# Gated delta rule in a two-block fp32 model: three pairs' token transposes moved into the first substitution, key products into the gate chain, 64x64 turns, and the merge copies in another order

## The reference, cut to what matters

```python
decay = jnp.exp(jnp.where(incl, gcum[..., :, None] - gcum[..., None, :], -jnp.inf))
a_kk = jnp.where(strict, jnp.einsum("bhnid,bhnjd->bhnij", k_beta, k) * decay, 0.0)
t_inv = lax.linalg.triangular_solve(eye + a_kk, eye, left_side=True, lower=True, unit_diagonal=True)
u = jnp.einsum("bhnij,bhnjd->bhnid", t_inv, v * beta[..., None])
w = jnp.einsum("bhnij,bhnjd->bhnid", t_inv, k_beta * jnp.exp(gcum)[..., None])
qk = jnp.einsum("bhnid,bhnjd->bhnij", q, k) * decay
...
v_new = ui - jnp.einsum("bhcd,bhde->bhce", wi, state)
o = jnp.einsum("bhcd,bhde->bhce", qd, state) + jnp.einsum("bhcj,bhje->bhce", qki, v_new)
state = state * gt[..., None, None] + jnp.einsum("bhcd,bhce->bhde", kd, v_new)
```

## Time and profile before

| what | us |
|---|---|
| runs | median 3757.83 of three, lowest 3757.76 |
| profiled execution, its own time | 3760.46 |
| its span, first to last instruction | 3758.6 |
| granted clock of PE, mean over the span | 0.97 of full speed (2.4 GHz) |
| delta rule of layer 0, from the gates (331 us) to the recurrence's first product (457 us) | 126 |
| the same in layer 1 | 1300 to 1427 |

### The profile page before, as it was taken

The page is one execution under the profiler, slowest core; times in us unless marked ns, Lnnn a source line. Parts: engine busy times, 40 slices in busy tenths (PEclk is TensorE's granted clock), DMA queues, the critical chain, the costliest instruction groups (busy, mean ns, idle before and its releaser), DMA issues.

```text
span 3758.6 us, 49965 instructions
## 1 busy us (share of the span) xinstructions
PE 3586.9 (95%) x18796; PEld 2882.4 (77%) x18796; DVE 1716.3 (46%) x2670; ACT 978.1 (26%) x1732; POOL 1819.9 (48%) x1049
## 2 busy tenths in 40 slices
PE   7999799999999979999999999999999999999999
PEld 5776677878776757787887788888888789888887
DVE  5255645737434574564551164444434124344342
ACT  3235532201223464121121133232101124232110
POOL 5522235656553222566565534435656431535654
PEclk9999799999999969999999989999999999999999
DMA  3211012323231101222222311213223423212222
GB/s 118 87 48 32 24 57 84 100 85 99 86 95 51 51 1 46 90 90 95 89 95 90 110 36 57 73 52 98 101 84 96 112 87 94 79 56 89 101 89 90
DMA packets 80743, 292.88 MB, mean 78 GB/s; under 512 B 8520, under 2 KB 9672, under 8 KB 80456
## 3 DMA queue, kind: packets, MB, share of 16 engines
q1 hardware_dynamic: 78496, 283.82, 23.7%
q10 hardware_dynamic: 1032, 2.62, 0.6%
q0 software_dynamic: 1056, 4.19, 0.3%
HBM read 281.69 MB, written 8.91 MB: 77 GB/s over the span
## 4 chain that ended last, share of the span: by engine, by line
PE 80%; DVE 9%; ACT 4%; issue 4%; DMA 1%; POOL 1%; DVEq 0%; ACTq 0%; SPq 0%; POOLq 0%
PE PSUM L337 19%; PE PSUM L336 19%; PE PSUM L335 19%; PE PSUM L896 2%; PE PSUM L1881 1%; PE PSUM L898 1%; PE PSUM L897 1%; DVE PSUM L494 1%; PE PSUM L1885 1%; DMA SLABS<-w_k 1%; PE PSUM L951 1%; DVE ACT_HI L1772 1%; PE PSUM L1459 1%; PE PSUM L908 1%; PE PSUM L1418 1%
## 5 line engine op out<-in xcount | busy, mean ns | idle before, releaser
L288 POOL TENSOR_TENSOR W_LOS<-SLABS,W_HI 128x1024 fp32r<-128x1024 f32 (+2 forms) x454 | 1157.7, 2550 | 37.9
L286 POOL TENSOR_SCALAR W_HI<-SLABS 128x1024 fp32r<-128x1024 f32 (+2 forms) x454 | 511.7, 1127 | 1316.6 <-DMA SLABS<-w_k 1316.6
L336 PE MATMUL PSUM<-H_LO,W_HI 128*128 128x512 f32 x2480 | 982.5, 396 | 0.0
L335 PE MATMUL PSUM<-H_HI,W_HI 128*128 128x512 f32 x2224 | 883.4, 397 | 26.1 <-DVE H_LO L479 20.9
L337 PE MATMUL PSUM<-H_HI,W_LOS 128*128 128x512 f32 x2224 | 884.7, 398 | 0.0
L336 PEld LDWEIGHTS PSUM<-H_LO,W_HI 128*128 128x128 f32 x2480 | 467.7, 189 | 118.2 <-issue 2.4
L335 PEld LDWEIGHTS PSUM<-H_HI,W_HI 128*128 128x128 f32 x2224 | 419.0, 188 | 131.8 <-issue 21.9
L337 PEld LDWEIGHTS PSUM<-H_HI,W_LOS 128*128 128x128 f32 x2224 | 418.5, 188 | 98.1
L494 DVE TENSOR_TENSOR PSUM<-PSUM,FACTORS 128x512 f32<-128x512 f32 x282 | 195.2, 695 | 554.0 <-PE PSUM L337 491.4
L335 PE MATMUL PSUM<-ACT_HI,W_HI 128*128 128x512 f32 x928 | 370.5, 399 | 13.0 <-DVE H_LO L455 6.4
L337 PE MATMUL PSUM<-ACT_HI,W_LOS 128*128 128x512 f32 x928 | 372.0, 401 | 0.0
(11 more groups left out here) (499 smaller groups left out, 5048.5 us busy)
## 6 DMA issues: line engine op xcount, KB each, us to landing
SLABS<-w_k SPq DMA_DIRECT2D x422, 512.0 KB, 3.5
SLABS<-w_k SPq DMA_DIRECT2D x32, 768.0 KB, 4.3
SLABS<-w_k SPq DMA_DIRECT2D x32, 640.0 KB, 3.9
ARENA<-gate_rows SPq DMA_DIRECT2D x8, 512.0 KB, 5.2
bias_rows<-SQ ACTq DMA_DIRECT2D x1, 2560.0 KB
X<-xT SPq DMA_DIRECT2D x1, 2048.0 KB, 8.4
gate_rows<-RT SPq DMA_DIRECT2D x8, 256.0 KB, 2.1
DX<-bias_rows POOLq DMA_DIRECT2D x8, 256.0 KB, 3.0
```

Of the source, the lines that this page charges most:

```text
L286: nc.gpsimd.tensor_scalar(hi, raw, 1.0, 0.0, MUL, ADD).then_inc(pool_step, 1)
L288: nc.gpsimd.tensor_tensor(lo, raw, hi.bitcast(F), SUB).then_inc(slab_split[s], 1)
L335: mm(out, w_hi, rhs[0](k), start=k == first, stop=False)
L336: mm(out, w_hi, rhs[1](k), start=False, stop=False)
```

## The change

1. **Key products of pairs 0 and 1** move out of the decay loop to the gate chain: pair 0's stand ahead of the row product, pair 1's where the second token transposes stood.
2. **Token transposes of pairs 1 to 3** move behind the query decays' spreading, so beside the first substitution; their values are now scaled and copied by ACT, in 8 instructions of 128 x 64 for a pair, and no more by DVE in one. Pair 0 stays, in other banks, and its value copy moves to DVE's part of the gate chain.
3. `BASE`'s negated rows are made by ACT from PSUM, and POOL's ones wait for one DVE pass less.
4. **Query squares** move from behind the diagonal copies into the decay loop (after pairs 1 and 2).
5. **Turns** become ordinary matmuls of 64 x 64 against the identity.
6. **Merge copies**: the diagonal blocks are written back for two pairs at a time, and behind the `x32` copies; for pairs 0 and 1 of the second direction DVE does it.

The diff, cut to its core:

```diff
@@ delta_prep_act
             nc.scalar.activation(ROWS_R[:], G_ROWS[:], ACT.Copy).then_inc(dn["gate_act"], 1)
+            nc.scalar.activation(BASE[64:96, :], G_ROWS[64:96, :], ACT.Copy, scale=-1.0).then_inc(dn["gate_act"], 1)
...
+        TOKEN_BANK = (0, 4, 6, 4)
@@ delta_prep_pe
             tokens_pe(pe, 0)
+            keys_pe(pe, 0)
             pe.wait_ge(*nth("cumx", 1))
...
-            tokens_pe(pe, 1)
+            keys_pe(pe, 1)
+
+        def products_pe(pe, p, bank, first):
+            for n in range(NCH):
+                for hh in range(2):
+                    h0, h1 = 64 * hh, 64 * hh + 64
+                    last = mm(tl(BANK[bank + hh], n), A(10 + p)[h0:h1, n * P:(n + 1) * P], A(first + p)[h0:h1, n * P:(n + 1) * P],
+                              start=True, stop=True)
+            last.then_inc(dn["kk"], 1)
@@ delta_prep_dve
+            value_tokens_dve(dve, 0)
...
-            nc.vector.tensor_scalar(BASE[64:96, :], hi[64:96, :], -1.0, None, MUL)
-            nc.vector.tensor_tensor(BASE[96:128, :], hi[96:128, :], G_ROWS[96:128, :], SUB)
+            nc.vector.tensor_tensor(BASE[96:128, :], hi[96:128, :], G_ROWS[96:128, :], SUB).then_inc(dn["base"], 1)
@@ delta_act
+            def value_tokens(p):
+                for n in range(NCH):
+                    for hh in range(2):
+                        c0, row = n * P + hh * 64, n * 8 + 2 * p + hh
+                        last = nc.scalar.activation(A(14 + p)[:, c0:c0 + 64], BANK[TOKEN_BANK[p] + 1][:, c0:c0 + 64], ACT.Copy,
+                                                    scale=KEY_NORM[:, row:row + 1])
+                last.then_inc(dn["vtok"], 1)
...
-                    if p == 0:
-                        key_tokens(2 + d)
-                if p + 2 < PAIRS:
-                    picks(p + 2)
+                if p in (1, 2):
+                    picks(p + 1)
+                    query_square(2 * p - 2)
+                    last = query_square(2 * p - 1)
...
+            for p in range(1, PAIRS):
+                key_tokens(p)
+                value_tokens(p)
...
             for d in range(2):
-                act.wait_ge(*nth("inv", INVERSE_COLS[d]))
-                for c in range(4):
-                    last = nc.scalar.activation(tiles(MAT[d], 32)[32 * c:32 * c + 32, :, 32 * c:32 * c + 32],
-                                                tiles(TTC, 32)[32 * c:32 * c + 32], ACT.Copy)
...
+                    if (d, p) != (1, 0):
+                        act.wait_ge(*nth("inv", INVERSE_COLS[d]))
+                        for c in range(4):
+                            last = nc.scalar.activation(*diagonal(d, p, c), ACT.Copy)
+                        last.then_inc(dn["diag"], 1)
@@ delta_pe
             for i in range(2 * PAIRS):
                 spread(i)
+            pe.wait_ge(*nth("m", 2 * PAIRS - 2))
+            tokens_pe(pe, 1)
             pe.wait_ge(*nth("m", 2 * PAIRS))
+            tokens_pe(pe, 2)
+            pe.wait_ge(*nth("gpe", 5))
             pe.wait_ge(*nth("qsq", 1))
...
+            tokens_pe(pe, 3)
...
                         for k in range(8):
-                            last = nc.tensor.transpose(tl(pair2(b + 1), k), tl(mat(q, d), k), C("ident"))
+                            last = mm(tl(pair2(b + 1), k)[h0:h0 + 64, h0:h0 + 64], tl(mat(q, d), k)[h0:h0 + 64, h0:h0 + 64],
+                                      C("ident")[h0:h0 + 64, h0:h0 + 64], start=True, stop=True)
@@ delta_dve
+            dve.wait_ge(*nth("inv", INVERSE_COLS[1]))
+            for c in range(4):
+                last = nc.vector.tensor_copy(*diagonal(1, 0, c))
+            last.then_inc(dn["diag"], 1)
@@ delta_pool
-            pool.wait_ge(*nth("row_lo", 1))
+            pool.wait_ge(*nth("base", 1))
```

More of the change, by code:

```diff
@@ L161, in build @@
             "logit", "exps", "gates", "gtok_psum", "cum_psum", "gate_act", "cols", "cumx", "row_psum", "row_lo",
[L162 removed]
+            "rows", "tok_psum", "ktok", "vtok", "pick_a", "pick_v", "diff", "base", "decay", "scaled", "kk", "m", "qk", "gp", "gpe",
             "qd", "kd", "unit", "inv", "diag", "x32_psum", "x32", "t32_psum", "t32", "turn_psum", "turn", "x64_psum", "x64",
@@ L1198, in first_half, with diag_blocks, diagonal @@
             return (0, 64) if d == 0 else (64, 0)
-        INVERSE_ROWS, INVERSE_COLS, TURNED_IN, DIAG_BLOCKS = (1, 4), (2, 5), 3, (3, 4)
+        INVERSE_ROWS, INVERSE_COLS, TURNED_IN = (1, 4), (2, 5), 3
+        def diag_blocks(d, p):
+            return nth("diag", 3 + 2 * d + p // 2)
+        def diagonal(d, p, c):
+            return (tiles(MAT[d], 32)[32 * c:32 * c + 32, 8 * p:8 * p + 16, 32 * c:32 * c + 32],
+                    tiles(TTC, 32)[32 * c:32 * c + 32, 8 * p:8 * p + 16, :])
         def delta_act(act):
@@ L1324, in decays @@
                 last.then_inc(dn["diff"], 1)
-            def products(p, bank, first):
-                for n in range(NCH):
-                    for hh in range(2):
-                        h0, h1 = 64 * hh, 64 * hh + 64
-                        last = mm(tl(BANK[bank + hh], n), A(10 + p)[h0:h1, n * P:(n + 1) * P], A(first + p)[h0:h1, n * P:(n + 1) * P],
-                                  start=True, stop=True)
-                last.then_inc(dn["kk"], 1)
-            def keys(p):
-                if p >= 2:
-                    pe.wait_ge(*nth("m", 2 * p - 2))
-                else:
-                    pe.wait_ge(*nth("ktok", p + 3))
-                    pe.wait_ge(*nth("vtok", p + 3))
-                products(p, 4 + 2 * (p % 2), 10)
             def queries(p):
@@ L1345, in queries @@
                 else:
-                    pe.wait_ge(*nth("qrow", 1))
-                products(p, 6, 6)
+                    pe.wait_ge(*nth("vtok", PAIRS))
+                products_pe(pe, p, 6, 6)
             def spread(i):
@@ L1487, in picks @@
                 last.then_inc(dn["pick_v"], 1)
-            values(0)
             dve.wait_ge(*nth("rows", 1))
-            picks(0)
-            picks(1)
-            values(1)
-            picks(2)
-            picks(3)
-            values(2)
-            values(3)
+            dve.wait_ge(*nth("base_hi", 1))
+            for p in range(PAIRS):
+                picks(p)
             for p in range(PAIRS):
```

79 lines of the change are left out of this document (40 added, 39 removed).

## The result

The changed kernel takes 3798.34 us in the median of four runs (3789.51 to 3811.98), against 3757.8 for the kernel before: a ratio of 1.0111, 95% interval [1.0094, 1.0128]. Run again with another set of the kernel before beside it, it gave 3800.3 and 1.0114 [1.0088, 1.0139]. That is 41 us more, where 21 were forecast with 3793 as the upper end; at 1.1% it stays under the 2% from which the forecast would call it slower. One of the four runs of the kernel before took 4464.11 us, the other three 3751.91 to 3757.83. The profiled execution took 3789.51 us, its span is 3787.7, the mean granted clock 0.956 of 2.4 GHz (before 0.970).

The account below looks back on a forecast made before the run. PE, busy 95% of the span, was taken to bound the kernel; +7.1 to the recurrence and +3.5 at its start made +10.6 us a layer, +21 for two, so 3779 us; own range 3768 to 3790, 8 in 10 3742 to 3793.

Parts of the forecast that it names:

- The gate chain's term of 0: Gate chain to first decay: -0.4 and -0.7 against +1.1 us sum to 0; bounds -0.5 and +1.1.
- The weighed rule: Merges: a skill's rule that transposes don't engage the full clock; the forecast held that the rows speak against it.
- Rivals 1: Merges: the clock rises as before with 64x64 turns; -6.4 us a layer, 3745 us; chance 0.25.
- rival 4: Recurrence: never gets back to full speed in its first group; at most +27 us a layer, 3830 us; chance 0.03.
- Rival 2: Decay loop: the clock falls before the first decays; +5.5 us a layer on top, 3790 us; chance 0.12.
- Rival 3: Merges, second direction: query products raise the clock; -7 us a layer, 3765 us; chance 0.13.
- ACT's overrun: Beside the first substitution: ACT is free at 396.4, the first x32 ready at 394.6; a new wait of 1.8 us.
- Layer 1 repeats layer 0, so each term counts twice: Whole sum: layer 0's +10.6 us was taken for both layers, +21 us.
- 2.1 for the squares: Before DVE's start: the squares no longer stand between ACT's diagonal copies, -2.1 us a layer.
- the loop's term: Decay loop: last exponential at 361.5 instead of 362.46, -1.0 us; ends -4.2 and +4.5.
- Recurrence start +3.5: Recurrence: starts at 1.2 GHz, 7 us at half speed, +3.5 us a layer; ends 0 and +4.4.
- The query products, 1.75 in my sum: Merges: first query products take 1.1 us fast, 1.1 to 2.2 at 1.2 GHz; 1.75 taken.

Follow-up runs that it names:

- wide_transposes: The changed kernel, but with the turns of the kernel before, eight 128x128 transposes for a unit: 3755.47 us, 0.9990 of the kernel before.
- wide_products: The changed kernel, but with each turn an ordinary 128x128 product with the identity: 3772.2 us, 1.0039 of the kernel before.
- loop_narrow: The changed kernel, 64x64 turns kept, plus 7 full-array products in each of the decay loop's two waits for picked rows: 3782.17 us, 1.0077 of the kernel before.
- dve_order_loop: The changed kernel with 128x128 transposes as turns, 7 full-array products in each decay-loop wait, and DVE writing back all the second direction's inverted blocks: 3755.66 us.

## Why the prediction was wrong

In layer 0 the mechanism was the forecast's, and its steps can be laid beside the trace (us):

| step | forecast | measured |
|---|---|---|
| last exponential ends | 361.5 | 360.34 |
| DVE starts | 366.4 | 365.35 |
| ACT free for the first x32 | 396.4 | 395.47 |
| first turns | 401.3 | 400.51 |
| second direction's first x32 | 428.9 | 428.07 |
| its turns | 432.6 | 432.01 |
| second turns | 451.9 | 452.46 |
| recurrence | 464.3 | 465.44 |

**Right.** Every step is within 1.2 us, but that closeness is partly luck. The forecast put the first decay at 340.6, and it came at 339.09, because the work ahead of the gate chain was 1.6 us shorter in this profile. Counted from the first decay, the recurrence was forecast 123.7 us on and came 126.35 on, 2.7 later. The gate chain's term of 0 was right (8.8 us in both kernels). The weighed rule came out as the rows had it. With turns of 128x128 transposes the clock comes back in the merges (`wide_transposes`), and with the same turns as ordinary products it does as well (`wide_products`). The Trainium skill (TensorE: Matmul & The Clock Gate, Part 4: PE-mode transpose) says that the full clock doesn't engage for transposes; `wide_transposes`, 3755.47 us and at 1.00 behind its turns, against 3798.34 us and 0.50 with 64x64 products, disagrees with it. Rivals 1 and 3 are out: query products and 64x64 turns run at 0.50 for the whole 90 us. So is rival 4, for the recurrence's first group ends at 1.00. Rival 2 has its place in layer 1: there the clock was up at the first decay but fell 2 us behind it, and the last exponential ended 25.1 us behind the first decay (1354.18 less 1329.07), where my forecast had 20.9 and the rival 26.4. In layer 0 it was 21.25. Rival 3's price doesn't follow from its own terms (twice 2.7 and 3.5 make 8.9 a layer, not 7). ACT's overrun, 1.8 in my sum, was 1.6: PE had the first unit's x32 at 393.8, half of the 1.92 behind 392.86, and ACT was free at 395.47.

**Wrong, in the order of size.**

- "Layer 1 repeats layer 0, so each term counts twice". In layer 1 the stage took 12.1 us more in the first profile, where layer 0 took 9.8, and the forecast had 7.1 in both. The merges alone cost 12.3 and 10.8. The other part, from the first decay to the first x32, is 2.5 less than before in layer 0 and 1.3 more in layer 1 (53.8 and 57.6 against 56.3), where the forecast had 3.1 less in both: 1.0 for the decay loop and 2.1 for the squares. The ends of the loop's term, -4.2 and +4.5, covered both, but I took the middle twice. To the end of the last exponential the loop itself was 0.5 shorter in layer 0 and 3.3 longer in layer 1, for there the clock fell 7 us earlier, behind the wait ahead of the first decay (2.49 us). The loop's own wait of 2.33 us, behind which it fell in layer 0, was in the forecast, without a price of its own. `loop_narrow` bridges that one, and both its loops are 3.8 us shorter. Why the clock falls at another place in layer 1 isn't shown; the second profile has it in the same place.
- "Recurrence start +3.5". It was 5.2 in either layer (4.9 once in the second profile), and beyond my end of 4.4. The half-speed stretch went on at least to 477, so 11.6 us behind its start instead of 7.
- The query products, 1.75 in my sum, take 2.0 at 1.2 GHz (from 435.58 to 437.59). There are three on the path behind the second direction's start: 0.8 of the 1.9 by which the table drifts from -0.8 to +1.1. Another 0.5 are the second direction's two pairs of turns, 3.57 us each until the next product starts (432.01 to 435.58) where I had 3.3.
- What lies outside the stage, but for the recurrence's start, counted as nothing. The outside holds 16 of the 39 us, some 10 of them the two slow starts, so 6 are left. One place in the rest can be read. In the stage behind layer 0, PE waits for DVE's last split before the down projection, 4.08 us in the first profile after and 4.05 in the second, against 0.89 and 0.91 before. DVE and POOL of the kernel before, then of the kernel after:

```profile
764.75 1.75 DVE L1774 TENSOR_TENSOR ACT_LO<-VF,ACT_HI 128x512 f32 x1
```

```profile
764.28 1.68 POOL L286 TENSOR_SCALAR W_HI<-SLABS 128x1536 fp32r<-128x1536 f32 x1 [0.77 <-DMA SLABS<-w_k]
```

```profile
781.16 3.78 DVE L1797 TENSOR_TENSOR ACT_LO<-VF,ACT_HI 128x512 f32 x1
...
793.00 0.69 DVE L1797 TENSOR_TENSOR ACT_LO<-KTOK,ACT_HI 128x512 f32 x1
```

```profile
780.84 3.55 POOL L288 TENSOR_TENSOR W_LOS<-SLABS,W_HI 128x1536 fp32r<-128x1536 f32 x1
```

The same instruction takes 0.69 with POOL idle (793.00). Beside POOL's it ends 0.55 us behind that one: 784.94 against 784.39. Which of POOL's instructions it meets seems to depend on how the two streams have shifted, and PE's wait of 4 us then costs the clock on top (the product behind it takes 0.80 instead of 0.50). In layer 1 the same wait was 4.13 us in the first profile of the kernel before and 0.59 in the second; after, it was 0.64 and 4.24. So it looks like an accident of alignment that any change of some us can bring or remove; that the change brings it in layer 0 every time isn't settled by two profiles. No experiment moved it by itself.

The step that failed is thus the sum. Its 21 us were 14.2 for the two stages and 7.0 for the two starts. Measured were 22.8 and some 10, of the 39 between the profiles: 2.7 too little in layer 0's stage and 5.9 in layer 1's, where "each term counts twice" failed at the decay loop, and 3 in the starts. The remaining 6 lie in the 3530 us outside the two stages, for which neither sum nor range held anything, though two executions of one kernel differ there by up to 12.8 us; what causes them stays open. The upper end of 3793 fell 5 us short.

## What to carry to other kernels

Before you replace a matmul by a smaller one, see what else it does: on this chip and in this kernel the wide, seemingly wasteful turns were what brought PE back to 2.4 GHz within the merges, and saving 0.3 us a pair, by my sum, cost 11 to 12 us a layer in the merges and 5 in what follows. Look at the granted clock of the stretch before and behind each wait, since a wait of 2 to 4 us that an edit moves onto PE can cost its length and then a slow stretch, as in the decay loop and in `dve_order_loop`. And a mean over several executions, by parts of the program, tells more than one profile: parts that nobody edited moved by up to 12.8 us here.
